# A two-block transformer on one core: the second mixer's last branch and its gates, the expert routing, and the overflow branch at the end, put in another order

## The reference

```python
def mixer_block(x, w_in, b_gate, rpb, sink, w_branch_na, w_branch_sw, w_out):
    ...
    y_na = y_na @ w_branch_na
    y_sw = y_sw @ w_branch_sw
    gates = jax.nn.sigmoid((gate_logits + b_gate).astype(jnp.float32)).astype(x.dtype)
    g_na, g_sw = jnp.split(gates, N_BRANCHES, axis=-1)
    return (g_na * y_na + g_sw * y_sw) @ w_out

def moe_swiglu(x, w_router, w_gate, w_up, w_down):
    logits = (xt @ w_router).astype(jnp.float32)
    top_vals, top_idx = lax.top_k(logits, TOP_K)
    top_w = jax.nn.softmax(top_vals, axis=-1)
    ...
    for e in range(N_EXPERTS):
        y = y + combine[:, e:e + 1] * swiglu(xt, w_gate[e], w_up[e], w_down[e])
    return y.reshape(B, S, D)

def second_block(...):
    x = layer_norm(x, emb_ln_g, emb_ln_b)
    for layer in range(DEPTH):
        m = mixer_block(...)
        x = layer_norm(DEEPNORM_ALPHA * x + m, ln1_g[layer], ln1_b[layer])
        f = swiglu(...) if layer % 2 == 0 else moe_swiglu(...)
        x = layer_norm(DEEPNORM_ALPHA * x + f, ln2_g[layer], ln2_b[layer])
```

## Time and profile before

| what | us |
|---|---|
| median of 3 runs | 2305.82 |
| lowest, highest | 2305.18, 2308.26 |
| the profiled execution, its own time | 2309.2 |
| its span in the trace | 2307.4 |
| its mean granted clock | 0.983 |

### The profile page before, as it was taken

How to read it: one execution, slowest core, us unless ns; L and a number is a source line. 1 busy time by engine, 2 the same in 40 slices (tenths; PEclk the granted TensorE clock), 3 DMA queues, 4 the chain that set the end, 5 groups by cost and what they waited for, 6 DMA issues and landing times.

```text
span 2307.4 us, 30965 instructions
## 1 busy us (share of the span) xinstructions
PE 2220.8 (96%) x11546; PEld 1875.0 (81%) x11546; DVE 1711.6 (74%) x2451; ACT 1483.5 (64%) x2169; POOL 229.1 (10%) x140
## 2 busy tenths in 40 slices
PE   8889999899998998999999899999999999999996
PEld 7878888787887897888888788888888888888885
DVE  6866556866555547555646699999999999999998
ACT  6655446665444564444465478777878777888886
POOL 1430000340002241000251000000000000000000
PEclk9999999999999999999999899999999999999998
DMA  7425555425555544655544499999999999999996
GB/s 280 136 82 202 187 189 194 142 65 191 189 188 192 167 131 148 205 186 189 191 151 132 142 356 368 353 363 346 369 349 371 357 358 356 367 364 375 366 376 226
DMA packets 157276, 570.89 MB, mean 247 GB/s; under 512 B 18560, under 2 KB 18912, under 8 KB 156480
## 3 DMA queue, kind: packets, MB, share of 16 engines
q1 hardware_dynamic: 154032, 555.58, 68.6%
q0 software_dynamic: 3088, 13.27, 1.7%
HBM read 567.72 MB, written 1.05 MB: 246 GB/s over the span
## 4 chain that ended last, share of the span: by engine, by line
PE 73%; DVE 4%; ACT 1%; issue 1%; POOL 1%; DVEq 0%; POOLq 0%; ACTq 0%
PE bank L503 20%; PE bank L505 20%; PE bank L504 19%; PE bank L2183 3%; PE bank L2185 3%; PE bank L2184 3%; PE bank L1801 1%; PE bank L1058 1%; DVE X L2053 1%; PE bank L2749 1%; PE bank L1073 1%; DVE w_lo L442 1%; PE bank L1000 1%; PE bank L2680 0%; DVE X L2012 0%
## 5 line engine op out<-in xcount | busy, mean ns | idle before, releaser
L442 DVE TENSOR_TENSOR w_lo<-raw,w_hi 128x1024 fp32r<-128x1024 f32 x990 | 1192.5, 1223 | 292.0 <-ACT w_hi L436 261.4
L436 ACT CAST w_hi<-raw 128x1024 fp32r<-128x1024 f32 x1055 | 1101.5, 1051 | 320.7 <-PE bank L505 266.2
L503 PE MATMUL bank<-w_hi,x_hi 128*128 128x512 f32 (+2 forms) x2144 | 838.5, 391 | 21.7 <-DVE x_lo L2084 7.9
L505 PE MATMUL bank<-w_hi,x_lo 128*128 128x512 f32 (+2 forms) x2144 | 827.6, 386 | 0.0
L504 PE MATMUL bank<-w_lo,x_hi 128*128 128x512 f32 (+2 forms) x2144 | 826.9, 386 | 0.0
L503 PEld LDWEIGHTS bank<-w_hi,x_hi 128*128 128x128 f32 x2144 | 406.6, 190 | 102.2 <-POOL w_lo L442 8.5
L505 PEld LDWEIGHTS bank<-w_hi,x_lo 128*128 128x128 f32 x2144 | 406.6, 190 | 79.1
L504 PEld LDWEIGHTS bank<-w_lo,x_hi 128*128 128x128 f32 x2144 | 407.2, 190 | 73.5
L442 POOL TENSOR_TENSOR w_lo<-raw,w_hi 128x1024 fp32r<-128x1024 f32 x65 | 155.4, 2394 | 581.9 <-ACT w_hi L436 577.0
L505 PE MATMUL bank<-w_hi,qk_l 128*128 128x512 f32 (+1 forms) x496 | 191.4, 386 | 0.0
L503 PE MATMUL bank<-w_hi,qk_l 128*128 128x512 f32 x448 | 178.1, 398 | 0.5 <-DVE w_lo L442 0.5
(11 more groups left out here) (280 smaller groups left out, 2031.1 us busy)
## 6 DMA issues: line engine op xcount, KB each, us to landing
raw<-in_stream SPq DMA_DIRECT2D x1055, 512.0 KB, 5.7
tab<-in_lngb POOLq DMA_DIRECT2D x5, 1024.0 KB, 8.5
arena<-in_rpb POOLq DMA_DIRECT2D x16, 256.0 KB, 7.2
tab<-in_rowv POOLq DMA_DIRECT2D x2, 640.0 KB, 10.1
X<-in_x SPq DMA_DIRECT2D x1, 1024.0 KB, 5.1
out_y<-X SPq DMA_DIRECT2D x4, 256.0 KB, 2.1
tab<-in_ropec POOLq DMA_DIRECT2D x2, 448.0 KB, 5.3
tab<-in_ropes POOLq DMA_DIRECT2D x2, 448.0 KB, 7.7
```

The costliest lines, as they stand in the source:

```text
L436: nc.scalar.copy(w_hi[:, s % SPLIT, :], raw[:, slot, :]).then_inc(hi_done, 1)
L442: e.tensor_tensor(w_lo[:, s % SPLIT, :], raw[:, s % RAW, :], w_hi[:, s % SPLIT, :].bitcast(F32), ALU.subtract).then_inc(done, 1)
L503: pe.matmul(out, xh, wh, start=first, stop=False)
L505: return pe.matmul(out, xl, wh, start=False, stop=last)
```

## The change

- The third and fourth `sw_half` are merged into `sw_last`, which waits for both weight halves and then adds both to bank 0, to bank 1, and so on; a bank's `sw_full` comes after its twelve matmuls.
- The gates are cut into `gate_mul`, `gate_add`, `gate_hi` and `gate_lo`, written between the half steps of the branch and of the output product.
- The router's logits go by units of four blocks, high parts first, and wait for high and low parts apart. TensorE's wait for the split router moves from the mixer to the first logits. One of VectorE's three splits behind the crossing now stands ahead of the second transposes' low parts, one behind them, one behind the gather.
- The mask is made first, as fp32r, against a copied fp32r table `counts`; the weights' arithmetic stands behind it. Two matmuls give the positions, two more the counts. Positions take one instruction, with `iota` raised by one beforehand; expert 0's selection follows at once, its weights and the flag after that.
- Gate and up of expert 0 wait for each gathered piece by itself; the piece with its weights comes after them (`first_weights`).
- The last `turn` stands between the two `down` halves before it, with buffers of its own. `last_down` does the left columns of both last halves, then the right ones; `output` takes the left columns on `left_full`.
- VectorE branches ahead of the last `output`; TensorE and ScalarE have the usual case first, and the second round in an `Else`. The three splits and loads beyond the stream's end are made in the second round alone.
- `final_norm` centres both token blocks before it scales either.

The diff, moved left by eight columns and cut where it only carries declarations and repeats:

```diff
@@ -485,6 +490,8 @@
+        elif self.st.s + AHEAD >= TOTAL:
+            pass
         elif self.kind == "act":
             split_hi(self.e, self.st, AHEAD)
         elif self.kind == "dve" and self.st.s + AHEAD not in POOL_LO:
+    def last_down(hT):
+        if E.kind == "pe":
+            s = E.st.s
+            e.wait_ge(ht_lo, E.ff.at())
+            for c in range(2):
+                w = slice(c * 512, (c + 1) * 512)
+                for hx in range(2):
+                    if c == 0:
+                        e.wait_ge(*lo_ready(s + hx))
+                    wh, wl = w_hi[:, (s + hx) % SPLIT, w], w_lo[:, (s + hx) % SPLIT, w]
+                    i = mm3(e, bank[4 + c][:, :], hT[0][:, hx, 0:T], hT[1][:, hx, 0:T], wh, wl,
+                            False, hx == 1)
+                    if c == 1:
+                        i.then_inc(w_used, 1)
+                if c == 0:
+                    i.then_inc(left_full, 1)
+            E.st.s += 2
+        else:
+            E.half_step()
+            E.half_step()
     def chunk(first=False, step=None, free=False):
...
                 for hx in range(4):
+                    if E.kind == "pe" and not (x or c):
+                        e.wait_ge(xe_lo, hx + 1)
                     gu_half(hx, t0=buf * P, b0=b0, free=x == 0 and c < 2, xs=x_sets[x // 2 % 2])
                     if hx == 1 and (x or c):
                         turn(c, pieces)
+                if not (x or c):
+                    first_weights(E)
...
-                if x or c:
+                if x == chain - 1 and c == nc_ - 1:
+                    ends = (hT_hi[:, :, P:2 * P], hT_lo[:, :, P:2 * P])
+                    down(0, False, False)
+                    E.ff.n += 1
+                    turn(hT=ends)
+                    E.ff.n -= 1
+                    down(1, False, False)
+                elif x or c:
                     down(0, c == 1, c == 0)
                     down(1, c == 1, c == 0)
...
-        turn()
-        down(0, False, True)
-        down(1, False, True)
-        output(E, chain, (chain + 1) % 4)
+        last_down(ends)
...
     if E.kind == "pe" and routed:
-        e.wait_ge(tp_lo, base + 2)
-        logits(E, 0)
+        logits(E, 0, base)
...
-    if E.kind != "pe" and part is not None:
+    if E.kind != "pe" and part is not None or later:
         E.half_step()
     tb_blocks(E, 1, (6, 7))
     if later:
-        for _ in range(left):
-            E.half_step()
+        E.half_step()
...
     for tb in range(TB):
         ln_mid(E, tb)
+    for tb in range(TB):
         ln_last(E, tb)
...
@@ -2367,7 +2402,26 @@
             e.wait_ge(ot_lo, n_pair + 2 * N_NA)
-        branch_half((0, 1, 2, 3), N_NA + k, k == 0, k == N_NA - 1, sw_full if k == N_NA - 1 else None)
+        branch_half((0, 1, 2, 3), N_NA + k, k == 0, False)
+    def sw_last():
+        for s in (E.st.s, E.st.s + 1):
+            e.wait_ge(*lo_ready(s))
+        for bk in range(4):
+            for k in (N_NA - 2, N_NA - 1):
+                s = (E.st.s + k - N_NA + 2) % SPLIT
+                for j in (0, 1):
+                    w = slice((2 * bk + j) * P, (2 * bk + j + 1) * P)
+                    i = both3(bank[bk][:, j * S:(j + 1) * S], w_hi[:, s, w], w_lo[:, s, w],
+                              OT_hi[:, N_NA + k, :], OT_lo[:, N_NA + k, :], False,
+                              k == N_NA - 1 and j == 1)
+                if bk == 3:
+                    i.then_inc(w_used, 1)
+            if bk < 3:
+                i.then_inc(sw_full, 1)
+        E.st.s += 2
     def na_gates(at):
-    def gated(j):
+    def gate_mul(j, end):
+        g = GT[:, KD + 2 * j:KD + 2 * j + 2, :]
+        e.wait_ge(gate_done, 2 * l + 2)
+        if j < 3:
+            e.wait_ge(sw_full, 3 * l + j + 1)
+        else:
+            e.wait_ge(w_used, end)
+        E.link(e.tensor_tensor(g, bank[j][:, :].rearrange("p (b n) -> p b n", n=S), g, ALU.mult))
+    def gate_add(j):
+        e.tensor_tensor(z, z, g, ALU.add).then_inc(yg_src, 1)
+    def gate_hi(j):
+        e.wait_ge(yg_src, (KD // 2) * l + j + 1)
+        nc.scalar.copy(x_hi[:, 2 * j:2 * j + 2, :], GT[:, 2 * j:2 * j + 2, :]).then_inc(yg_hi, 1)
+    def gate_lo(j):
+        e.wait_ge(yg_hi, (KD // 2) * l + j + 1)
+        e.tensor_tensor(x_lo[:, b, :], GT[:, b, :], x_hi[:, b, :].bitcast(F32),
+                        ALU.subtract).then_inc(yg_lo, 1)
...
-        sw_half(k)
-    for j in range(KD // 2):
-        gated(j)
-    for k in range(4):
-        out_half(k)
+    end = E.st.done(N_NA - 1)
+    sw_half(0)
+    sw_half(1)
+    if E.kind == "pe":
+        sw_last()
+        for k in range(4):
+            out_half(k)
+    elif E.kind == "act":
+        E.half_step()
+        gate_hi(0)
+        E.half_step()
+        gate_hi(1)
+        E.half_step()
+        gate_hi(2)
+        E.half_step()
+        gate_hi(3)
+        E.half_step()
+        E.half_step()
+    elif E.kind == "dve":
+        gate_mul(0, end)
+        gate_add(0)
+        gate_mul(1, end)
+        gate_lo(0)
+        E.half_step()
+        gate_add(1)
+        gate_mul(2, end)
+        gate_lo(1)
+        E.half_step()
+        gate_add(2)
+        gate_mul(3, end)
+        gate_lo(2)
+        E.half_step()
+        gate_add(3)
+        E.half_step()
+        gate_lo(3)
+        E.half_step()
+        E.half_step()
+    else:
+        for _ in range(N_NA + 2):
+            E.half_step()
-    if E.kind == "pe":
-        e.wait_ge(rw_split, 2)
+        e.wait_ge(route_in, 32)
+        e.tensor_copy(counts[:, :, :], tab[:, 2 * D:2 * D + 2 * P].rearrange("p (a n) -> p a n", a=2))
+        E.link(e.tensor_scalar(iota[:, :], iota[:, :], 1.0, None, ALU.add))
...
+    if tb == 0:
+        E.e.wait_ge(rw_split, 2)
-    for k in range(KD):
-        E.e.matmul(o, x_hi[:, k, t], rw[:, k, :], start=k == 0, stop=False)
-        i = E.e.matmul(o, x_lo[:, k, t], rw[:, k, :], start=False, stop=k == KD - 1)
+    o = bank[3][:, tb * 2 * NE:(tb + 1) * 2 * NE]
+    for u in range(2):
+        for x, made in ((x_hi, tp_hi), (x_lo, tp_lo)):
+            E.e.wait_ge(made, n + u + 1)
+            for k in range(4 * u, 4 * u + 4):
+                i = E.e.matmul(o, x[:, k, t], rw[:, k, :], start=x is x_hi and k == 0,
+                               stop=x is x_lo and k == KD - 1)
...
+        e.memset(CW, 0.0)
+        e.memset(POS, 0.0)
         e.wait_ge(lg_full, 1)
...
-        e.tensor_tensor(v3(oh1), io, x3[:, :, 1:2].to_broadcast([P, TB, 8]), ALU.is_equal)
+        E.link(e.tensor_tensor(v3(oh1), io, x3[:, :, 1:2].to_broadcast([P, TB, 8]), ALU.is_equal))
+        e.tensor_tensor(msk[:, :], oh0, oh1, ALU.add).then_inc(route, 1)
         e.tensor_tensor(dv.unsqueeze(2), m3[:, :, 1:2], m3[:, :, 0:1], ALU.subtract).then_inc(top_done, 1)
         e.wait_ge(exp_done, 1)
         E.link(e.tensor_scalar(w1, ev, 1.0, None, ALU.add))
         E.link(e.reciprocal(w0, w1))
         E.link(e.tensor_tensor(w1, w0, ev, ALU.mult))
-        e.memset(CW, 0.0)
-        E.link(e.memset(POS, -1.0))
...
+        e.wait_ge(route, 1)
+        e.matmul(bank[2][:, 0:16], counts[:, 0, :], msk[:, :], start=True, stop=False, skip_group_check=True)
+        e.matmul(bank[2][:, 8:16], counts[:, 1, :], msk[:, 0:8], start=False, stop=True,
+                 skip_group_check=True).then_inc(pos_full, 1)
+        e.matmul(bank[3][:, 32:40], counts[:, 1, :], msk[:, 0:8], start=True, stop=False)
+        e.matmul(bank[3][:, 32:40], counts[:, 1, :], msk[:, 8:16], start=False, stop=True).then_inc(pos_full, 1)
+    if E.kind == "dve":
+        e.wait_ge(pos_full, 1)
+        E.link(e.scalar_tensor_tensor(ps3, bank[2][:, 0:16].rearrange("p (t n) -> p t n", t=TB), 1.0, v3(MSK),
+                                      ALU.add, ALU.mult))
+        for tb in range(TB):
+            i = e.tensor_scalar(SE[:, tb, :], iota[:, 0:P], POS[:, tb * XW:tb * XW + 1], None, ALU.is_equal)
+        i.then_inc(se_ready, 1)
...
-        e.tensor_tensor(MSK, oh0, oh1, ALU.add).then_inc(route, 1)
...
-        e.wait_ge(route_in, 32)
-        e.wait_ge(route, 1)
-        e.matmul(bank[2][:, 0:8], tri[:, :], MSK[:, 0:8], start=True, stop=True)
-        e.matmul(bank[2][:, 8:16], ones[:, :], MSK[:, 0:8], start=True, stop=False)
-        e.matmul(bank[2][:, 8:16], tri[:, :], MSK[:, 8:16], start=False, stop=True)
-        e.matmul(bank[2][:, 16:24], ones[:, :], MSK[:, 0:8], start=True, stop=False)
-        e.matmul(bank[2][:, 16:24], ones[:, :], MSK[:, 8:16], start=False, stop=True).then_inc(pos_full, 1)
-    if E.kind == "dve":
-        e.wait_ge(pos_full, 1)
-        E.link(e.tensor_scalar(ps3, bank[2][:, 0:16].rearrange("p (t n) -> p t n", t=TB), 1.0, None, ALU.add))
-        E.link(e.tensor_tensor(ps3, ps3, v3(MSK), ALU.mult))
-        E.link(e.tensor_scalar(ps3, ps3, -1.0, None, ALU.add))
-        E.link(e.tensor_reduce(cntm[:, 0:1], bank[2][:, 16:24], AX.X, ALU.max))
+        for tb in range(TB):
+            i = e.tensor_copy(cw_in[:, tb:tb + 1], CW[:, tb * XW:tb * XW + 1])
```

(70 more changed lines are left out.)

53 lines of the change are left out of this document (21 added, 32 removed).

## The result

Medians: 2283.18 us after (2281.81 to 2285.07, 4 runs), 2306.29 before (2305.18 to 2308.26, 4 runs); ratio 0.9902, 95% interval 0.9889 to 0.9914. The prediction said 2284.6 in a range of 2278 to 2295. The profiled execution of after took 2285.07 us, its span 2283.2, its mean granted clock 0.987; beside that of before it is 24.1 us shorter, where the steps made 21.2. The medians are 23.1 us apart.

What follows compares the result with a forecast made beforehand. TensorE, busy for 96% of the span, was taken as the bound, so gains come only where it idles or runs at the lower clock. Terms sum to 21.2: 2305.8 - 21.2 = 2284.6 us, range 2278 to 2295.

Steps and rivals of the forecast that it cites:

- part 1: Last branch and gates, both mixers: idle and lower clock at the output halves go, 2 x 3.9 = 7.8 us.
- part 2: First mixer's start: TensorE's wait for the split router goes, 1.8 us idle and 1.4 of clock; 3.2 us.
- part 3: Routing: logits start earlier 1.2, reduction to gather shorter 3.9, wait behind the gather gone 0.4; 5.5 us.
- part 4: Last chunk: earlier turn gains 1.0, VectorE's branch stall partly hidden, 1.3 us of it staying; 4.2 us in all.
- part 5: Final norm: the second centring fills VectorE's 0.54 us idle for GpSimd's root; 0.5 us.
- Rivals D and E: Mixer gates: D, they don't hide, 2292.4 us, chance 0.04; E, nothing in their chain overlaps, 2317, chance 0.02.
- Rival B: First mixer's start gives nothing, a split or the clock taking the wait's place; 3.2 us less, 2287.8; chance 0.08.
- Rival A: VectorE's branch stall at the end stays on the path; takes 3 of 4.2 us, 2287.6; chance 0.14.
- Rival C: Clock drops at other crossings as work moves; 2279.6 to 2289.6 us; chance 0.12 as the main deviation.
- One sign named as wrong: Among the signs that would show the forecast wrong: an expert stretch longer than 972.9 us.
- that stretch moves as a block and keeps its length: Experts: the stretch of 972.90 us, TensorE busy for 972.14 of it, was to move without changing length.

Runs made afterwards that it cites:

- p1_mix_old: The changed kernel with the old order of last branch halves, gates and output halves put back in both mixers; 2291.36 us.
- p2_rw_wait: The changed kernel with TensorE's wait for the split router put back in the first mixer; 2285.51 us.
- pad4: The changed kernel with four unused VectorE operations (2.86 us) ahead of the second `gate_add`; 2285.84 us in one run.
- p3_logits_wait: The changed kernel with the router's logits waiting for both low parts again before their first matmul; 2285.81 us.
- dve_fall: The changed kernel with VectorE's two branches on the overflow flag made into one, the usual arm first; 2285.07 us.
- no_round2: The changed kernel without the second round for overflowing experts, and without reading the flag or branching on it; 2284.33 us.
- p4_branch_late: The changed kernel with VectorE's branch behind the last output's low parts instead of ahead, flag still loaded ahead; 2288.89 us.
- p3_route_old: The changed kernel with routing as before from the reduction on, the logits kept as changed; 2289.36 us.
- warm: The changed kernel with 14 matmuls of 512 columns that compute nothing added in routing; 2283.59 us.

## Why the prediction was right

| step | forecast | measured | by |
|---|---|---|---|
| part 1, twice | 7.8 | 8.3 | p1_mix_old, 2 x 4.16 |
| part 2 | 3.2 | 3.5 | 1.9 at the mixer's start, 1.6 behind it (profiles; 2.0 by p2_rw_wait) |
| part 3 | 5.5 | 6.7 | 5.7 to the gather, 1.0 behind its start |
| part 4 | 4.2 | 4.6 | turn's place 0.8, branch's 1.5, the rest below |
| part 5 | 0.5 | 0.5 | centring to result, 5.88 to 5.38 (profiles alone) |
| end behind the last result | 0 | 0.6 | 3.65 to 3.02, the last store's landing |
| dense feed-forward | 0 | -1.5 | a drop of the clock |
| experts | 0 | -2.2 | 0.5 matmuls moved in, the rest pitch |
| first crossing to end | 21.2 | 20.6 | profiles |
| ahead of the first crossing | 0 | 3.6 | same code |

**Part 1** held in mechanism and size: idle gone, clock 1.00 over the 10.9 us behind. The covers were 0.3 to 0.8 us better than worked out. Rivals D and E are out; pad4 shows how near they were: it took 2.86 us on VectorE to make 1.3.

**Part 2**: 1.8 of idle as in the earlier trace rows, put back by p2_rw_wait as 2.0. The 1.4 us for the clock came in the comparison of the two profiles, but not in the run that puts the wait back; it belongs to where the drop fell, and that it comes with the wait is not shown. Of the 3.2 forecast, about 2 are the change's for certain. Rival B is out.

**Part 3**: reduction to gather took 3.27 where 3.5 was worked out and 7.36 was before. The two under-sized terms are the logits (1.6 for 1.2: TensorE began them at once, and p3_logits_wait gives 1.63) and what lies behind the gather's start (1.0 for 0.4). Of that 1.0 some 0.5 is no gain: the prediction says that `first_weights` only moves, and its four matmuls moved from this stage into the next, where they cost the same.

**Part 4**: the turn 0.8 for 1.0. The second sum starts 7.52 us after the turn. The turn stands six matmuls (1.36 us) earlier than before, so counted from its old place it is 6.16; before it was 2295.27 - 2284.54 = 10.73, so 4.57 for 4.17. That the stall is hidden in part was right: against dve_fall and no_round2, after has 1.0 us of its 3.1 exposed ahead of the low part, where 1.3 was the forecast, and 0.7 in most kernels with the same tail, where the stall is 2.8. Only 0.6 of it reach the last sums, as TensorE's scatter and the right columns bound them next. Putting the branch back costs 1.45 at the second sum. What remains of the 4.57, some 2.3 us, is the rest of the order (the three splits gone from VectorE ahead of the low parts, left columns before right ones); it was not tried by itself.

**Rival A** is out on both counts: the stall moved with the jump (p4_branch_late, dve_fall), and the second conditional's branch took 50 ns, with the low part 0.1 us behind. The Trainium skill's page Runtime: NRT & Kernel Launch, under Instruction fetch mechanics, says that a taken branch to code outside the fetched window waits for its fetch. The runs agree: the jump over the second round is followed by 2.8 to 3.2 us without work, and the branch in dve_fall, whose arm stands right behind it, held up nothing. The Trainium skill's page Advanced Engine Details and Errata, under Control Flow Timing, gives a compare-and-branch about 108 ns; the records here are 50 and 76 ns, and the wait behind a jump is no part of that figure.

**Rival C** came true on both sides at once, so part of the total's nearness is luck. The clock fell 12 times in before's profile and 10 times in after's. The dense feed-forward lost 1.5 by a drop, the part ahead of the first crossing gained 3.6 by an earlier rise and shorter drops. Since that part is the same code and other kernels of this study stand at 722.5 to 723.9 there as before does, the 3.6 us are no merit of the change; in medians it may hold some of the 1.4 us by which the result beat the forecast.

**One sign named as wrong did show**: experts longer than 972.9 us. 973.71 with the turn earlier, 974.86 like for like, in every new kernel, almost without idle (busy 972.90 of 973.71) and at clock 1.00. So the step "that stretch moves as a block and keeps its length" failed, by 2.0 us. Of these, 0.5 come 5.6 us behind the experts' start, where the four matmuls of `first_weights` now stand (1296.55 in after; in before they stood at 1311.19, ahead of the experts' first matmul at 1311.66). The other 1.5 us come at 0.1 to 0.3 per expert: the same matmuls follow each other a little more slowly. Neither the code's length (no_round2), nor routing (p3_route_old), nor part 1 changes this, and its cause stays open. The 2.0 us are 0.1% of the run and a tenth of the forecast gain.

## What to carry to other kernels

Cost an island of idle together with the clock behind it, but book the clock's part as chance: a run that puts the wait back tells the two apart. Judge a part by its own stage in the trace, where 0.1 us can often be seen, not by totals in which identical code varies by 3.6. Where a branch skips a long body, put it where its engine waits anyway; putting the usual case right behind the branch brought the last stores forward by 0.55 us and gave no time here, as the last one took longer to land. When work moves over the border of a stage, move its cost in the sum too: the 0.5 us of `first_weights` looked like a gain in one stage and a loss in the next.

## What the runs showed that was not expected

- Code that is the same in both kernels took 720.3 to 723.9 us in fourteen profiles. Between before and after, 1.1 of the 3.6 us arise at the start, where the clock rose to 1.00 for the next 60 us at 18.7 instead of 16.4 us, 1.1 at the half-clock interval at 80 us and some 1.4 at that at 485 us (6.8 us long each, against 3.4). The five profiles with 722.5 us or more are those whose interval at 79 to 81 us lasted 6.8 us; the sum of the half-clock intervals doesn't order them (from 79 us on 27 us in p3_route_old with 722.8, 24 in p2_rw_wait with 720.7, 24 in warm with 722.5).
- With matmuls that compute nothing, put where TensorE waits, the granted clock stayed up: 0.90 instead of 0.67 over routing, and a 3.1 us shorter stretch for 14 of them. From the first crossing on up to 4.7 us went in the profiles (of them 1.4 that other kernels have without dummies), and nothing that the medians could show.
- The same 1.83 us of idle was followed by a drop of the clock in before and by none in p2_rw_wait. In both the clock had been down shortly ahead of the idle, until 10.3 and 9.1 us before it began, so that does not tell them apart.
- A jump over VectorE's second round was followed by 2.8 to 3.2 us without work in twelve profiles, while the record of the branch itself takes 76 ns.
- The last store took 2.1 us to land without any branches (no_round2), 2.6 to 2.9 in most kernels, and 3.2 and 3.35 in before and dve_fall. What sets this is open, and it ate what dve_fall gained ahead of it.
